# Latent attention stage: key and value compression ahead of the query's, norm chains and side products moved between units

## The reference, cut to what matters

```python
p = h @ w_in
c_q, c_kv, k_pe = jnp.split(p, (Q_RANK, Q_RANK + KV_RANK), axis=-1)      # 384, 256, 64
q = (_rmsnorm(c_q, q_a_norm) @ w_q_up).reshape(B, T, MLA_HEADS, QK_DIM)  # 8 heads of 192
kv = (_rmsnorm(c_kv, kv_a_norm) @ w_kv_up).reshape(B, T, MLA_HEADS, NOPE_DIM + V_DIM)
k_nope, v = kv[..., :NOPE_DIM], kv[..., NOPE_DIM:]
k = jnp.concatenate([k_nope, jnp.broadcast_to(k_pe[:, :, None, :], (B, T, MLA_HEADS, ROPE_DIM))], axis=-1)
q = _rmsnorm(q, q_norm)
k = _rmsnorm(k, k_norm)
q = jnp.concatenate([q[..., :NOPE_DIM], _rope(q[..., NOPE_DIM:], cos, sin)], axis=-1)
k = jnp.concatenate([k[..., :NOPE_DIM], _rope(k[..., NOPE_DIM:], cos, sin)], axis=-1)
o = _causal_attention(q, k, v)
return o.reshape(B, T, MLA_HEADS * V_DIM) @ w_out
```

## Time and profile before

| what | value |
|---|---|
| median of 3 runs | 2674.83 us (2672.76 to 2674.86) |
| the profiled execution's own time | 2673.86 us |
| its span, first to last instruction | 2672.1 us |
| mean granted TensorE clock | 0.977 |
| compression units of the stage start at | 2009 us of the span |
| twenty units start at | 2054.7 us |
| first head's value product starts at | 2176.3 us |

### The profile page before, as it was taken

How to read it: one execution, slowest core, us unless ns; L and a number is a source line. 1 busy time by engine, 2 the same in 40 slices (tenths; PEclk the granted TensorE clock), 3 DMA queues, 4 the chain that set the end, 5 groups by cost and what they waited for, 6 DMA issues and landing times.

```text
span 2672.1 us, 36150 instructions
## 1 busy us (share of the span) xinstructions
PE 2567.5 (96%) x13941; PEld 1966.0 (74%) x13941; DVE 1251.6 (47%) x1582; ACT 845.6 (32%) x1143; POOL 1192.5 (45%) x601
## 2 busy tenths in 40 slices
PE   8999999899999998889999999999999999999999
PEld 7666678688888766776788887888886446788887
DVE  7999775533322588564433223333226463433301
ACT  5422343432222334223322223222223223422221
POOL 3799824444444455213444444444443201344443
PEclk9999999899999999999999999999999979999999
DMA  5222223233333322002233333333332201233332
GB/s 144 71 71 72 67 67 104 70 89 92 94 94 94 104 71 58 6 4 83 83 92 93 96 90 97 94 94 93 89 94 74 72 0 32 84 92 92 92 95 80
DMA packets 417607, 212.85 MB, mean 80 GB/s; under 512 B 16773, under 2 KB 415931, under 8 KB 417499
## 3 DMA queue, kind: packets, MB, share of 16 engines
q1 hardware_dynamic: 414475, 209.05, 27.0%
q10 hardware_dynamic: 3024, 2.30, 0.4%
HBM read 209.22 MB, written 2.10 MB: 79 GB/s over the span
## 4 chain that ended last, share of the span: by engine, by line
PE 85%; POOL 7%; DVE 6%; ACT 2%; issue 1%; DMA 0%; ACTq 0%; POOLq 0%; DVEq 0%
PE bank L339 22%; PE bank L332 22%; PE bank L336 22%; PE bank L1334 3%; PE bank L1335 3%; PE bank L1336 3%; POOL w_lo L312 2%; PE bank L2107 2%; PE bank L2608 1%; PE bank L2607 1%; PE bank L2643 1%; PE bank L2560 1%; POOL tmp L787 1%; PE bank L2566 1%; POOL ph_sin L771 1%
## 5 line engine op out<-in xcount | busy, mean ns | idle before, releaser
L312 POOL TENSOR_TENSOR w_lo<-w_raw,w_hi 128x1024 fp32r<-128x1024 f32 (+3 forms) x420 | 976.5, 2326 | 1321.8 <-ACT w_hi L303 1320.0
L303 ACT ACTIVATE w_hi<-w_raw 128x1024 fp32r<-128x1024 f32 (+3 forms) x420 | 425.0, 1013 | 1419.3 <-PE bank L339 1230.0
L332 PE MATMUL bank<-hH,w_hi 128*128 128x512 f32 x1792 | 472.2, 404 | 19.4 <-ACT hH L469 8.4
L336 PE MATMUL bank<-hL,w_hi 128*128 128x512 f32 x1792 | 459.6, 398 | 0.9 <-DVE hL L374 0.9
L339 PE MATMUL bank<-hH,w_lo 128*128 128x512 f32 x1792 | 454.6, 395 | 1.0 <-POOL w_lo L312 0.9
L332 PEld LDWEIGHTS bank<-hH,w_hi 128*128 128x128 f32 x1792 | 339.1, 189 | 118.2 <-ACT w_hi L303 13.2
L336 PEld LDWEIGHTS bank<-hL,w_hi 128*128 128x128 f32 x1792 | 340.0, 190 | 85.5 <-DVE hL L374 2.2
L339 PEld LDWEIGHTS bank<-hH,w_lo 128*128 128x128 f32 x1792 | 335.7, 187 | 83.7 <-POOL w_lo L312 1.8
L524 DVE TENSOR_TENSOR tmp<-bank,R 128x512 f32<-128x512 f32 x88 | 60.9, 692 | 400.3 <-PE bank L339 400.2
L530 DVE TENSOR_TENSOR ffn_aL<-tmp,ffn_aH 128x512 f32 (+1 forms) x88 | 155.8, 1770 | 86.3 <-ACT ffn_aH L491 86.3
L336 PE MATMUL bank<-ffn_aL,w_hi 128*128 128x512 f32 x704 | 179.8, 395 | 0.0
(11 more groups left out here) (470 smaller groups left out, 2704.5 us busy)
## 6 DMA issues: line engine op xcount, KB each, us to landing
w_raw<-in_ffn_w_gate SPq DMA_DIRECT2D x88, 512.0 KB, 3.8
w_raw<-in_ffn_w_up SPq DMA_DIRECT2D x88, 512.0 KB, 3.8
w_raw<-in_ffn_w_down SPq DMA_DIRECT2D x64, 512.0 KB, 3.6
w_raw<-in_w_in SPq DMA_DIRECT2D x48, 512.0 KB, 3.7
w_raw<-in_even_w_in SPq DMA_DIRECT2D x26, 512.0 KB, 3.8
w_raw<-in_ffn_w_down SPq DMA_DIRECT2D x32, 384.0 KB, 3.2
w_raw<-in_w_conv_out SPq DMA_DIRECT2D x8, 512.0 KB, 3.7
w_raw<-in_w_out SPq DMA_DIRECT2D x8, 512.0 KB, 3.6
```

The source lines that it names most:

```text
L303: nc.scalar.activation(w_hi[u % 2][:, 0:K, :], w_raw[u % 4][:, 0:K, :], ACT.Identity).then_inc(w_hi_ready, 1)
L312: nc.gpsimd.tensor_tensor(w_lo[u % 2][:, 0:K, :], w_raw[u % 4][:, 0:K, :], w_hi[u % 2][:, 0:K, :].bitcast(F32), ALU.subtract).then_inc(w_l ...
L332: nc.tensor.matmul(out, H[:, k, :], sH[:, k0 + k, :], start=start and k == 0, stop=False)
L336: nc.tensor.matmul(out, H[:, k, :], sL[:, k0 + k, :], start=False, stop=False)
```

## The change

- The compression units run in the order key and value tile 0, 1, rope tile, query tile 0, 1, 2.
- The key compression's sum of squares stands after the fourth unit, its root, reciprocal, scaling and high and low parts beside the fifth and sixth; the rope spread stands after the fifth. The high and low parts get buffers of their own.
- Of the twenty units the eight key units come first, then the four rope units of the queries, then the eight others of the queries. The query compression's sum stands after the second key unit, its norm chain beside the next ones.
- Side products get one numbered list `SIDE`: beside key units 2 to 5 four value products, beside units 9 to 12 the turns, beside units 12 to 19 the eight key spreads, and behind head 0's scores the last four value products. The copies of those stand behind head 0's maxima on VectorE.
- The root and the reciprocal of the key sums stand beside units 8 and 9; the small transposes of the query sums stand between head 0's second and third score tile.

The new functions `c_sum`, `c_root`, `c_norm`, `c_hi`, `c_low`, `k_rope` and `side` hold operations that were written out before. The number of matrix products, activations, vector operations and loads is the same. The diff, cut to its core:

```diff
@@ -232,15 +232,15 @@
         U_F.append(n)
         n += FFN_UNITS
         U_OI = n
-        n = plan(n, col_units(wview(IN["odd_w_in_2"][0]), 8, [P * j for j in range(5)] + [576]))
-        U_QN = n
...
+        n = plan(n, col_units(wview(IN["odd_w_in_2"][0]), 8, [384, 512, 576, 0, P, 2 * P]))
+        U_KN = n
         wkv = wview(IN["mla_w_kv_up_2"][0])
         n = plan(n, col_units(wkv, 2, [256 * h for h in range(8)]))
+        U_QP = n
+        wq = wview(IN["mla_w_q_up_2"][0])
+        wq_heads = IN["mla_w_q_up_2"][0].rearrange("(k p) (h c) -> p k h c", p=P, c=192)
+        n = plan(n, [(wq_heads[:, :, 2 * q:2 * q + 2, 128:192], 3) for q in range(4)])
+        n = plan(n, col_units(wq, 3, [192 * h for h in range(8)]))
...
+        OI_TILE = (3, 4, 5, 0, 1, 2)
+        SIDE = [("k_rope", 0), ("k_rope", 1)] + [("v", n_) for n_ in range(4)] + [("turn", p_) for p_ in range(4)]
+        SIDE += [("key", h) for h in range(AH_)] + [("v", n_) for n_ in range(4, 8)]
+        def side_no(what, i):
+            return SIDE.index((what, i)) + 1
+        def side_bank(what, i):
+            return bank[7 - side_no(what, i) % 2]
+        def sum_no(m_):
+            return m_ + 1 if m_ < 8 else m_ + 2
...
+            def c_square(n_):
+                act.wait_ge(group_read, G_OF[U_OI] + n_ + 1)
+                dst = (tmp[0], tmp[1], pe_sq, tmp[2], tmp[3], tmp[5])[n_]
+                s.activation(dst[:, :], cc[:, OI_TILE[n_], :], ACT.Square).then_inc(mla["c_sq"], 1)
...
+            split_hi(act, U_OI + 2)
+            root_act(act, D, EPS6)
+            split_hi(act, U_OI + 3)
+            split_hi(act, U_OI + 4)
+            c_square(0)
+            c_square(1)
+            split_hi(act, U_OI + 5)
+            c_square(2)
+            for t_, d_ in ((1, sinr), (2, cosr)):
+                act.wait_ge(mla["angle"], t_)
+                s.activation(d_[:, :], rt[t_][:, :], ACT.Sin).then_inc(mla["table"], 1)
+            c_root(0, kdup, 256)
+            split_hi(act, U_OI + 6)
+            c_square(3)
+            c_hi(cvH, 3, 0)
+            c_square(4)
+            split_hi(act, U_OI + 7)
+            c_square(5)
+            for m_ in range(20):
+                u = U_KN + m_
                 split_hi(act, u + 2)
...
+                if m_ >= 3:
+                    act.wait_ge(mla["ss_mm"], sum_no(m_ - 3))
+                s.activation(tmp[m_ % 3][:, :], bank_of(u)[:, :], ACT.Square).then_inc(mla["sq"], 1)
+                if m_ == 1:
+                    c_root(1, tmp[4], 384)
+                elif m_ == 5:
+                    c_hi(cqH, 0, 2)
+                elif m_ == 8:
+                    act.wait_ge(mla["ss_mm"], 9)
+                    s.activation(rk8[0:8, :], bank[5][0:8, :], ACT.Sqrt, scale=1.0 / QK, bias=small[0:8, 0:1]).then_inc(mla["k_root"], 1)
...
+            def c_norm(g_, rr, js, gname):
+                v.wait_ge(mla["c_root"], g_ + 1)
+                V.reciprocal(rr[:, :], rr[:, :]).then_inc(dve_step, 1)
+                v.wait_ge(dve_step, dve_sent(dve_step))
...
+            for n_ in range(6):
+                j = OI_TILE[n_]
+                v.wait_ge(unit_done, U_OI + n_ + 1)
+                V.tensor_tensor(cc[:, j, :], bank_of(U_OI + n_)[:, :], R[:, :], M).then_inc(group_read, 1)
                 v.wait_ge(group_read, dve_sent(group_read))
-                if j == 1:
+                if n_ == 3:
+                    v.wait_ge(mla["c_sq"], 3)
+                    V.tensor_scalar(cc[:, 5, :], cc[:, 5, :], pc("kn_pe"), None, M).then_inc(mla["pe_gain"], 1)
+                    c_norm(0, kdup, range(3, 5), "kva")
+                elif n_ == 4:
+                    c_low(cvL, cvH, 3, 0)
...
+            for m_ in range(20):
+                u = U_KN + m_
+                dst, gain = ((kn[:, m_, :], "kn") if m_ < 8 else (qp[:, m_ - 8, :], "qn_pe") if m_ < 12
+                             else (qn[:, m_ - 12, :], "qn"))
+                v.wait_ge(mla["sq"], m_ + 1)
                 V.tensor_scalar(dst, bank_of(u)[:, :], pc(gain), None, M).then_inc(group_read, 1)
                 dve_sent(group_read)
...
+                if m_ == 1:
+                    k_rope()
+                if m_ == 3:
+                    c_norm(1, tmp[4], range(3), "qa")
+                if 2 <= m_ < 6:
+                    v_out(m_ - 2)
+                if m_ == 5:
+                    c_low(cqL, cqH, 0, 2)
+                if m_ == 9:
+                    v.wait_ge(mla["k_root"], 1)
+                    V.reciprocal(rk8[0:8, :], rk8[0:8, :]).then_inc(mla["rk"], 1)
+                    dve_sent(mla["rk"])
+                if 9 <= m_ < 13:
+                    turn_q(m_ - 9)
+                if m_ >= 12:
+                    k_scale(m_ - 12)
...
             maxes(0, range(TT))
+            for n_ in range(4, 8):
+                v_out(n_)
...
+            def c_sum(g_, tiles, first):
+                for n_, t_ in enumerate(tiles):
+                    pe.wait_ge(mla["c_sq"], first + n_ + 1)
+                    ins = mm(bank[5 - g_][:, :], ones[:, :], t_[:, :], start=n_ == 0, stop=n_ == len(tiles) - 1)
+                ins.then_inc(mla["c_ps"], 1)
+            def side(what, i):
+                n_ = side_no(what, i)
+                if n_ >= 3:
+                    pe.wait_ge(mla["side_rd"], n_ - 2)
+                out = side_bank(what, i)[:, :]
+                if what == "k_rope":
+                    pe.wait_ge(mla["pe_gain"], 1)
+                    ins = mm(out, omask[:, 2 + i, :], cc[:, 5, :], start=True, stop=True)
+                elif what == "v":
+                    for k in range(2):
+                        ins = mm(out, cc[:, 3 + k, (i // 2) * P:(i // 2 + 1) * P], wv[:, k, (i % 2) * T:(i % 2 + 1) * T],
+                                 start=k == 0, stop=k == 1)
+                elif what == "turn":
+                    pe.wait_ge(group_read, G_OF[U_QP] + i + 1)
+                    ins = mm(out, omask[:, 1, :], qp[:, i, :], start=True, stop=True)
+                else:
+                    pe.wait_ge(mla["rk"], 1)
+                    ins = mm(out, ident[0:8, i:i + 1].to_broadcast([8, P]), rk8[0:8, :], start=True, stop=True)
+                ins.then_inc(mla["side_ps"], 1)
...
+                elif n_ == 3:
+                    c_sum(0, (tmp[0], tmp[1]), 0)
+                elif n_ == 4:
+                    side("k_rope", 0)
+                    side("k_rope", 1)
+            pe.wait_ge(mla["sel"], 1)
+            pe.wait_ge(lsem, 64)
+            for m_ in range(20):
+                if m_ < 8:
+                    unit(pe, U_KN + m_, 2, cvH, cvL, ready=(mla["c_lo"], 0) if m_ == 0 else None)
                 else:
...
+                if m_ == 1:
+                    c_sum(1, (tmp[2], tmp[3], tmp[5]), 3)
+                if m_ == 8:
+                    pe.wait_ge(mla["c_root"], 2)
+                if m_ >= 1:
+                    head_sum(m_ - 1)
+                if m_ == 8:
+                    mm(bank[5][0:8, :], bones[:, 64:72], pe_sq[:, :], start=False, stop=True).then_inc(mla["ss_mm"], 1)
+                if 2 <= m_ < 6:
+                    side("v", m_ - 2)
+                if 9 <= m_ < 13:
+                    side("turn", m_ - 9)
+                if m_ >= 12:
+                    side("key", m_ - 12)
...
-            scores(0, range(TT))
+            scores(0, range(2))
+            pe.wait_ge(mla["qs_rd"], 1)
+            for i in range(TT):
+                ins = tr(bank[4][:, i * AH_:(i + 1) * AH_], tmp[5][0:8, i * P:(i + 1) * P], ident[0:8, 0:8])
+            ins.then_inc(mla["qs_ps"], 1)
+            scores(0, range(2, TT))
+            for n_ in range(4, 8):
+                side("v", n_)
```

More of the change, by code:

```diff
@@ L2326, in odd_act @@
-            for g_, dim in ((0, 384), (1, 256)):
-                act.wait_ge(mla["c_ps"], g_ + 1)
-                s.activation((tmp[4], kdup)[g_][:, :], bank[4 + g_][:, :], ACT.Sqrt, scale=1.0 / dim, bias=EPS6).then_inc(mla["c_root"], 1)
-            for j in range(5):
-                act.wait_ge(mla["c_norm"], j + 1)
-                s.activation(ccH[:, j, :], cc[:, j, :], ACT.Identity).then_inc(mla["c_hi"], 1)
-            for n_ in range(20):
-                u = U_QN + n_
-                split_hi(act, u + 2)
-                if n_ >= 3:
-                    act.wait_ge(mla["ss_mm"], n_ - 2)
-                s.activation(tmp[n_ % 3][:, :], bank_of(u)[:, :], ACT.Square).then_inc(mla["sq"], 1)
@@ L2339, in odd_act, with c_root @@
-            act.wait_ge(mla["ss_mm"], 21)
-            s.activation(rk8[0:8, :], bank[5][0:8, :], ACT.Sqrt, scale=1.0 / QK, bias=small[0:8, 0:1]).then_inc(mla["k_root"], 1)
+            def c_square(n_):
+                act.wait_ge(group_read, G_OF[U_OI] + n_ + 1)
+                dst = (tmp[0], tmp[1], pe_sq, tmp[2], tmp[3], tmp[5])[n_]
+                s.activation(dst[:, :], cc[:, OI_TILE[n_], :], ACT.Square).then_inc(mla["c_sq"], 1)
+            def c_root(g_, dst, dim):
+                act.wait_ge(mla["c_ps"], g_ + 1)
```

(49 more changed lines are left out.)

151 lines of the change are left out of this document (40 added, 111 removed).

## The result

The changed kernel took 2647.81 us in the median of 4 runs (2646.12 to 2652.3), against 2674.85 for the kernel before; the ratio is 0.990, 95% interval 0.989 to 0.991. 2648.1 was forecast, in a range of 2644 to 2657. The profiled execution has a span of 2646.6 us, 25.5 less than before.

The account below looks back on a forecast made before the run. TensorE, busy nearly throughout, was taken as the bound, losing time to waits and slow clock. Its stretch shrinks from 131.7 to 104.0 us; 27.7 less 1.0 of waits gives 26.7, so 2648.1 us, range 2644 to 2657.

Parts of the forecast that it names:

- TensorE's own work: From the sixth compression unit to the first attention value product: 104.0 us at full clock after the change, against 131.7.
- query steps: Twelve query units with head sums, 39.1 us, plus one sum, four turns and eight key spreads, 11.2: together 50.3.
- small waits: Remaining waits allowed for in the reordered stage: 1.0 us, taken off the 27.7 us gain.
- Chain (a): Key compression's norm chain beside the last two compression units: 13.0 us under 15.0 of TensorE work, cost 0.
- fifth rival: Key compression chain outlasts its cover because ScalarE function changes cost more than the load's row: at worst 2652, chance 0.03.
- (b): Query compression's norm chain on VectorE beside the key units: second value copy 5.4 us late, cost 0, at worst 1 to 2.
- (c): Key norms' root and reciprocal beside the first query units: fits with 2 to 3 us to spare.
- (d): Join to the attention: first scores wait about 0.5 us for the last gain; cost 0 to 2, taken as 0.5.
- first rival: VectorE becomes the bound in places, reciprocals and scalings delaying bank-freeing copies: 8.8 us back, 2657, chance 0.13.
- 3.8 us wait: TensorE's wait for the reciprocal of the key norms (rk), said to leave 37 us behind it at 1.2 GHz.
- rival 2: Light work itself holds the clock down; head 0's scores and what follows at half clock: 19.8 us back, 2668, chance 0.07.
- cross-check: Second count of the stage's gain: waits 8.6, head of query units 1.7, half clock 17.6, together 27.9 us.

Follow-up runs that it names:

- fill_both: Kernel before, its wait for rk filled with four unread products and one unread full-row product behind each key spread: 2683.11 us, ratio 1.0025.
- longer_chain_a: Changed kernel with one more unread 3.35 us reciprocal in the key compression's norm chain on VectorE: 2651.0 us, timed once.
- fill_rk: Kernel before, with four unread f32 products put into TensorE's 3.8 us wait for rk: 2675.05 us, ratio 0.9995.
- spreads_behind: Changed kernel with the eight key spreads put back behind the last unit, rk ready long before: 2661.42 us, ratio to before 0.9951.
- spreads_128rows: spreads_behind with each key spread made a product over all 128 rows, the added rows zeros: 2650.77 us, ratio to before 0.9908.
- idle_scores: Changed kernel with TensorE made to wait about 3.8 us in front of head 0's first scores: 2660.47 us, timed once.
- spreads_twice: spreads_behind with each key spread issued twice in a row, so TensorE has no gap between them: 2674.05 us, timed once.
- idle_units: Changed kernel with TensorE made to wait about 3.8 us in front of the unit of step 14: 2648.98 us, timed once.

## Why the prediction was right, and where it was not

*TensorE's own work.* The terms, by start times in the trace after: side products among the compressions 3.4 (forecast 3.4); key units with sums and values 2049.52 to 2078.08, 28.6 (29.0); query steps to 2129.97, 51.9 (50.3); last sum 1.0 (0.9); head 0's scores, tiny transposes and late values 2130.93 to 2144.11, 13.2 (13.0); to the value product 6.8 (6.8). Together 104.9, against 104.0 and 1.0 for small waits. The query steps were under-priced: a step with a key spread takes 4.30 us, so a spread costs 1.04 and not 0.86. The turn, a product over 128 rows at the same place in the step, costs 0.84, so the difference goes with the eight rows. The spreads of fill_both, each between two products over 128 rows, have a period of 1.05 as well; what takes the time in such a change of rows isn't shown. A turn step and a spread step, by their head sums:

```profile
2084.49 1.03 PE L2617 MATMUL bank<-tmp,selp 128*8 128x512 f32 x2
...
2088.59 1.02 PE L2617 MATMUL bank<-tmp,selp 128*8 128x512 f32 x2
...
2102.15 1.02 PE L2617 MATMUL bank<-tmp,sel 128*8 128x512 f32 x2
...
2106.45 1.02 PE L2617 MATMUL bank<-tmp,sel 128*8 128x512 f32 x2
```

The microsecond of small waits did not come, so two errors cancel, and the closeness of the total is in that part luck. So is that of 2648.1 to 2647.81: the runs of the one kernel lie between 2646.12 and 2652.3.

*Chain (a).* Foreseen were 13.0 us under a cover of 15.0. Found were 13.1, from the end of the fourth compression unit at 2034.89, under 14.6:

```profile
2036.86 2.11 DVE L2440 TENSOR_SCALAR c_all<-c_all,par 128x512 f32<-128x512 f32 x1
2041.25 3.35 DVE L2421 RECIPROCAL k_rope_once<-k_rope_once 128x512 f32<-128x512 f32 x1 [2.28 <-ACT k_rope_once L2333]
2044.64 1.42 DVE L2424 SCALAR_TENSOR_TENSOR c_all<-c_all,par,k_rope_once 128x512 f32<-128x512 f32 x2
2045.97 0.68 DVE L2435 TENSOR_TENSOR c_all<-bank,R 128x512 f32<-128x512 f32 x1
2046.69 1.29 DVE L2431 TENSOR_TENSOR cv_lo<-c_all,cv_hi 128x512 fp32r<-128x512 f32 x2
```

The last low part ends at 2047.98, the first key unit starts at 2049.52; slack 1.5, and longer_chain_a confirms it: of 3.35 us added, 1.7 appear. The fifth rival did not come. ScalarE's two loads stand in the trace with nothing behind them; the second starts at 2039.24 and its root at 2040.53, the first and its sine are:

```profile
2036.77 1.28 ACT L2349 ACT_TABLE_LOAD   x1
2038.07 0.63 ACT L2349 ACTIVATE rope_sin<-rope_t 128x512 f32<-128x512 f32 x1
```

*Chains (b), (c), (d).* No wait of TensorE for v_rows, rk, or head 0's softmax; the first rival did not come. In (b) the copy of the second value product ends at 2070.11 and the fourth product starts at 2071.29, so 1.2 us were left of the 3.1 that the two steps seemed to give; the three scalings ahead of the copy took 2.55 where 2.08 was reckoned. The first scores did not wait for the last gain.

*The clock.* This is the step that failed in its reasoning, though not in its result. "The 3.8 us wait is the small part of its own cost: 37 us of work behind it ran at 1.2 GHz" names the wait as the cause; and rival 2, that the light work holds the clock down, was put at 0.07 because the clock had fallen before that work began. The fall in the wait was real, and it hid the second cause, the run of spreads over eight rows. With the wait filled the clock fell in the spreads and the time stayed (fill_rk, ratio 0.9995), with the wait absent it fell in the spreads (spreads_behind), and with full rows it did not (spreads_128rows). Of rival 2 the part on the scores is wrong: with the clock up they keep it up, with the clock down they do not raise it (idle_scores). The change removed both causes, and so the sum, which had only asked what the same products take at full clock, came out. That it took the spreads out of their run is luck as far as the prediction goes, which counts that move as relief from VectorE's pace, and units between the spreads only as help behind a new wait. With the wait gone but the spreads in one run the kernel gains 13.9 us in the stage (spreads_behind) and not 26.8.

*The cross-check* had 17.6 us of clock in the 37.0 and came to 27.9; its total is right and its division is not. spreads_128rows shows what that stretch is worth at full clock in its old order: 10.2 of spreads at VectorE's pace where 6.9 was reckoned. So 3.3 of the 17.6 were VectorE's pace, and the 1.7 of the first wait ScalarE's chain. The 26.8 us by the runs: 10.4 are the slow clock that eight-row spreads bring, 2.6 their pace behind the units, and 13.9 lie between spreads_behind and the kernel before. Of these, waits are 8.6 less the 1.3 that spreads_behind has of its own, 7.3; the head of the query units 1.7; and the clock was down for 35 us before (2139.3 to 2174.4) and for 27.2 in spreads_behind, whose late value products end it, worth (35.1 - 27.2)/2 = 4.0. Together 13.0; 0.9 stays open. The 4.0 are reckoned from the clock and not isolated by a run.

## What to carry to other kernels

Of a slow-clock stretch ask two questions: what took the clock down, and what of the work in it would take or keep it down alone; fill the wait ahead of it before giving it the whole blame. Products that use few rows of the array are best placed singly among full ones, or, where the moving tile can have zero rows, made full; in the order of spreads_behind that cost no time and gave 10.4 us. To price a reordered stage, add up the loop periods of the trace at full clock and give each norm chain a named cover: this came within 1 us over a stage of 140, though two errors of about a microsecond cancelled.

## What the runs showed of the hardware that was not expected

- A product over 8 rows and one over 128 rows of the same 512 columns have the same length in the trace, 1.12 us for a pair of records at 2.4 GHz (the changed kernel, spreads_128rows), yet in a run of the first the clock went down (spreads_behind, spreads_twice, fill_rk) and in a run of the second it did not (spreads_128rows), though the added rows are zeros and TensorE had gaps.
- After the fall, scores (half of them over 64 rows) ran for 11.4 us with TensorE busy and the clock did not rise; it rose 2.6 us (idle_scores) and 4.4 us (spreads_behind) into value products. In the kernel before, in fill_rk and in fill_both it rose behind a head's ten 128 x 128 transposes, at most 3 us after their end. The Trainium skill, TensorE: Matmul & The Clock Gate, Part 4: PE-mode transpose, says that transposes do not count as busy in the same way. The rows here lean against that, but no run isolates the transposes, since score products over all 128 rows follow them.
- The same 2.8 us wait ahead of the last head took the clock down in the kernel before, in the changed kernel and in nine of the other runs, and not in idle_units: from the first value product to the first output unit 64.3 to 65.0 us at clock 0.97 in the eleven, 63.3 at 1.00 in the one. So one trace of a wait does not settle what such a wait costs, by a microsecond or so. The runs do not say why.
- The gain of the rope tile, 128 x 512 in SBUF, took 2.11 us where it took 0.49 before, in the chain of (a) above. It ran beside a weight split of GpSimd and ended with it, at 2039.0 against 2038.7; before, no split ran beside it:

```profile
2036.29 2.40 POOL L312 TENSOR_TENSOR w_lo<-w_raw,w_hi 128x1024 fp32r<-128x1024 f32 x1 [3.19 <-ACT w_hi L303]
```

The Trainium skill, SBUF — State Buffer, section Who interferes with whom, says that VectorE, when it works in one of its two-port modes, and GpSimd exclude each other from a shared port pair, and that whoever issues first holds it for its whole instruction. The row agrees: the split started first, and the gain ended 0.3 us after it. In which mode the gain ran, no row tells. It cost nothing, as VectorE waited for the root 2.28 us afterwards.
